# State-space scan: PSUM banks given by purpose, and a step's within-tile outputs summed last

## The reference, cut to what matters

```python
acum = jnp.cumsum(dtc * A, axis=2)                                   # running sums
Lm = jnp.exp(jnp.where(causal, acum[:, :, :, None] - acum[:, :, None, :], -jnp.inf))
CB = jnp.einsum('bnigs,bnjgs->bnijg', Cc, Bc)                        # keys times queries
y_diag = jnp.einsum('bnijg,bnijgr,bnjgr,bnjgrp->bnigrp', CB, Lm, dtc, xc)   # within the tile
ds = jnp.einsum('bnjgr,bnjgrp,bnjgs->bngrps', wj, xc, Bc)            # what the tile adds to the state
y_off = jnp.einsum('bnigs,bngrps,bnigr->bnigrp', Cc, s_prev, jnp.exp(acum)) # from the state
y = y_diag + y_off
```

## Time and profile before

| what | value |
|---|---|
| median of 3 runs | 2664.28 us (2662.90 to 2666.83) |
| the profiled execution, its own time | 2660.27 us |
| its span, first to last instruction | 2658.3 us |
| PE busy | 2324.3 us, 87% of the span |
| DVE busy | 828.9 us, 31% |
| ACT busy | 565.8 us, 21% |
| POOL busy | 96.5 us, 4% |
| mean granted TensorE clock | 0.932 of full speed |

### The profile page before, as it was taken

One profiled execution on the slowest core, in us unless ns is written; L12 is line 12 of the kernel. 1 busy time (PEld: TensorE's weight loads), 2 busy tenths in 40 slices (PEclk: granted clock), 3 DMA queues, 4 the chain that ended last, 5 costly groups with the idle time before them and its releaser, 6 DMA issues. The chain is left out here.

```text
span 2658.3 us, 35179 instructions
## 1 busy us (share of the span) xinstructions
PE 2324.3 (87%) x14554; PEld 1406.2 (53%) x14554; DVE 828.9 (31%) x1447; ACT 565.8 (21%) x1160; POOL 96.5 (4%) x64
## 2 busy tenths in 40 slices
PE   6999999999887988988479999999998779799873
PEld 3546754754555545555335466547545555455542
DVE  1255512530635222110203653125206452321002
ACT  2133301410244121000021332033102540210000
POOL 0000000100021000000000000001000210000000
PEclk8999998999988998998789999989999889899996
DMA  6321052214301215999553211331243102179993
GB/s 252 111 97 64 1 190 80 79 64 158 127 20 45 95 38 218 402 419 420 219 212 112 81 56 50 141 111 48 89 143 132 48 1 94 38 282 413 420 420 134
DMA packets 136274, 407.01 MB, mean 153 GB/s; under 512 B 9446, under 2 KB 34534, under 8 KB 125352
## 3 DMA queue, kind: packets, MB, share of 16 engines
q1 hardware_dynamic: 122600, 388.37, 38.4%
q10 hardware_dynamic: 11776, 9.97, 1.1%
q0 software_dynamic: 1728, 6.29, 0.7%
HBM read 388.59 MB, written 16.02 MB: 152 GB/s over the span
## 5 line engine op out<-in xcount | busy, mean ns | idle before, releaser
L301 PE MATMUL ps<-hT,ring 128*128 128x384 f32 x1344 | 473.3, 513 | 57.7 <-ACT arena L1524 30.6
L301 PEld LDWEIGHTS ps<-hT,ring 128*128 128x128 f32 x1344 | 268.0, 202 | 251.3 <-issue 84.1
L301 PE MATMUL ps<-ring,hT 128*128 128x512 f32 x768 | 337.1, 600 | 3.9 <-PEq L1033 3.9
L301 PE MATMUL ps<-arena,ring 128*128 128x384 f32 x768 | 253.0, 492 | 11.4 <-DVE arena L499 5.1
L301 PEld LDWEIGHTS ps<-ring,hT 128*128 128x128 f32 x768 | 147.1, 193 | 192.2 <-issue 191.6
L301 PEld LDWEIGHTS ps<-arena,ring 128*128 128x128 f32 x768 | 146.9, 192 | 115.4 <-issue 17.2
L1807 PE MATMUL ps<-ring,arena 128*32 128x256 f32 x2432 | 147.4, 405 | 30.3 <-DMA ring<-in_e_w 25.8
L1807 PE MATMUL ps<-arena 128*32 128x256 f32 x2432 | 143.9, 398 | 25.9 <-DMA arena<-in_e_w 25.9
L333 PE MATMUL ps<-cst,arena 128*128 128x128 f32 x472 | 77.6, 313 | 75.0 <-DVE arena L2086 34.4
L1807 PEld LDWEIGHTS ps<-ring,arena 128*32 128x32 f32 x2432 | 89.2, 117 | 85.0 <-issue 38.5
L1807 PEld LDWEIGHTS ps<-arena 128*32 128x32 f32 x2432 | 86.6, 115 | 78.7 <-issue 36.5
(11 more groups left out here) (293 smaller groups left out, 2456.4 us busy)
## 6 DMA issues: line engine op xcount, KB each, us to landing
ring<-in_e_w SPq DMA_DIRECT2D x48, 2048.0 KB, 15.9
arena<-in_e_w SPq DMA_DIRECT2D x48, 2048.0 KB, 17.5
ring<-in_w_in SPq DMA_DIRECT2D x36, 2048.0 KB, 7.8
ring<-in_w_ada SPq DMA_DIRECT2D x24, 2048.0 KB, 8.1
ring<-in_a_wo SPq DMA_DIRECT2D x4, 2048.0 KB, 11.6
ring<-in_b_wo SPq DMA_DIRECT2D x4, 2048.0 KB, 8.1
ring<-in_c_wo SPq DMA_DIRECT2D x4, 2048.0 KB, 8.0
ring<-in_w_out SPq DMA_DIRECT2D x4, 2048.0 KB, 7.7
```

Source lines behind the costliest of these rows:

```text
L301: ins = pe.matmul(out, a, b, start=(i == 0), stop=(i == len(pairs) - 1))
```

## The change

Every claim in the scan names its bank: the four `ai` (and, before the steps, the input states `si`) take banks 0 to 3, the gate tile of the step after bank 4, `cb` bank 5, and `ds`, `yo`, `so` (and the sums `sc`) banks 6 and 7. The two `yd` take the banks of `cb` and the gate, 5 and 4. The two gate tiles after the last step still take the next bank in turn. On DVE, `yo` moves ahead of the four masks, and the two `yd` sums move behind the state update. No instruction is added or removed.

```diff
-        def gate_pe(pe, n, key, g):
+        def gate_pe(pe, n, key, g, bank=None):
...
-            matmuls(pe, claim(pe, ((key, i), j))[:, 0:T],
+            matmuls(pe, claim(pe, ((key, i), j), bank)[:, 0:T],
...
+            B_GATE, B_CB, B_DS = 4, 5, 6
...
-                    gate_pe(pe, W_GC, "gc", 0)
+                    gate_pe(pe, W_GC, "gc", 0, B_GATE)
...
-                            transposed(pe, ("si", d, q), [ssd_in[:, d, 4 * q + i, :] for i in range(4)])
+                            transposed(pe, ("si", d, q), [ssd_in[:, d, 4 * q + i, :] for i in range(4)], 2 * d + q)
...
-                        out = claim(pe, ("sc", d))
+                        out = claim(pe, ("sc", d), B_DS + d)
...
-                        out = claim(pe, ("cb", s))
+                        out = claim(pe, ("cb", s), B_CB)
...
-                            out = claim(pe, ("ai", s, q))
+                            out = claim(pe, ("ai", s, q), q)
...
-                                pe.matmul(claim(pe, ("yo", s, g)), xbc[:, 10 + g, col],
+                                pe.matmul(claim(pe, ("yo", s, g), B_DS + g), xbc[:, 10 + g, col],
...
-                            gate_pe(pe, W_GC, "gc", s + 1)
+                            gate_pe(pe, W_GC, "gc", s + 1, B_GATE)
...
-                                pe.matmul(claim(pe, ("ds", s, g)), b_tok[:, t, g, :],
+                                pe.matmul(claim(pe, ("ds", s, g), B_DS + g), b_tok[:, t, g, :],
...
-                            out = claim(pe, ("yd", s, g))
+                            out = claim(pe, ("yd", s, g), (B_CB, B_GATE)[g])
...
-                                transposed(pe, ("so", d, q), [ssd_p[:, 512 * q + P * i:512 * q + P * i + P] for i in range(4)])
+                                transposed(pe, ("so", d, q), [ssd_p[:, 512 * q + P * i:512 * q + P * i + P] for i in range(4)], B_DS + q)
...
                         dve.wait_ge(*read(("sc", d)))
-                        for r in range(4):
-                            dve.wait_ge(*following(dve, "decayed_ready"))
-                            dve.tensor_tensor(decayed[:, 4 * r:4 * r + 4, :], quad(diff[:, r % 2, :]),
-                                              each(cbm[s % 2][:, r // 2, :], 4), ALU.mult).then_inc(*counts("mask_ready"))
-                        if s + 1 < len(SCAN):
-                            masked_keys(s + 1)
                         for g in range(G_C):
                             out = y_c[:, t, 512 * g:512 * g + 512]
                             if t:
...
-                        for g in range(G_C):
-                            out = y_c[:, t, 512 * g:512 * g + 512]
-                            dve.wait_ge(*made(("yd", s, g)))
-                            dve.tensor_tensor(out, bank(("yd", s, g)), out, ALU.add).then_inc(*reads(("yd", s, g)))
-                            dve.wait_ge(*read(("yd", s, g)))
+                        for r in range(4):
+                            dve.wait_ge(*following(dve, "decayed_ready"))
+                            dve.tensor_tensor(decayed[:, 4 * r:4 * r + 4, :], quad(diff[:, r % 2, :]),
+                                              each(cbm[s % 2][:, r // 2, :], 4), ALU.mult).then_inc(*counts("mask_ready"))
+                        if s + 1 < len(SCAN):
+                            masked_keys(s + 1)
                         if s not in LAST:
...
+                        for g in range(G_C):
+                            out = y_c[:, t, 512 * g:512 * g + 512]
+                            dve.wait_ge(*made(("yd", s, g)))
+                            dve.tensor_tensor(out, bank(("yd", s, g)), out, ALU.add).then_inc(*reads(("yd", s, g)))
+                            dve.wait_ge(*read(("yd", s, g)))
                         if t == 0:
```

## The result

The changed kernel takes 2606.24 us in the median of 4 runs (2603.20 to 2613.03), the kernel before 2663.78 of 4: ratio 0.978, interval 0.9768 to 0.9792. The forecast was 2601, within 2589 to 2622. The profiled execution took 2605.94 us, its span is 2603.7, the mean granted clock 0.938 (before 2660.27, 2658.3, 0.932).

What follows compares the result with a forecast made beforehand. A chain between engines bounds the scan: PE's gate tile waits for a bank ACT reads behind DVE's masks. Saving 31.8 us a layer, 63.6 in all, takes 2660.27 to 2596.7; plus 4.01 gives 2601 us, range 2589 to 2622.

Steps and rivals of the forecast that it cites:

- The wait: Scan, PE before the gate tile: its bank waits for ACT's reading of q = 2, behind DVE's masks; 15.3 us in three waits.
- PE's part of a step: Scan step without a stall: gate start to `yd` 9.08 us, `yd` to `yo` 3.51, `yo` 1.9; sum 14.5.
- Steps 1 and 2: First-layer scan intervals between `yd` starts: `yd` from 754.68 to 768.5 in step 1, to 784.6 in step 2.
- The copies of `so`: Scan step 2: they follow the second `yd` sum for 1.42 us and hold `yo`, 2 us of waiting moved.
- The price of the collision: DVE's `yo` additions meeting POOL's products end 0.55 us after a product; the pairs end 4.75 after the second `yd` sum.
- The last mask: Scan step 5 on DVE: over at 826.5, in time for the second half of the last `yd`.
- The rule cited from the Trainium skill: A VectorE instruction with two SBUF inputs and a GpSimd instruction reading SBUF lock each other out; without it 2590 us.
- The lower bound: No collision of additions with POOL, 0.69 us each, and last `yd` 3.7 instead of 7.06: 5.5 a layer, 2590 us.
- Rival (b): Clock stays at 1.2 GHz: gate tiles of steps 1 to 4 take 8.08 instead of 5.33 us; 2623 us, chance 0.06.
- Rival (c): Slower: late `yd` sums hold banks 4 and 5, the gate waits for DVE's whole step; 2683 us, chance 0.03.
- the rest shifts whole: After the scan, PE's gate tiles and DVE's norm start from the last `yd` as today, keeping the 63.6 us saved.
- the 4.01 us: Amount by which the median of the runs lies above the profiled execution, added to 2596.7 for 2600.7 us.

Runs made afterwards that it cites:

- the wait put back: Changed kernel plus one PE wait ahead of the gate tile, in steps 1 to 4, for ACT's reading of the running sums of q = 2: 2659.51 us.
- banks alone: Changed kernel with DVE's order put back to masks, `yo`, `yd` sums, state update; banks by purpose stay: 2637.92 us, ratio 0.9891.
- sums last alone: Kernel before, banks still in turn, with only the `yd` sums moved behind the state update: 2639.94 us, ratio 0.9903.
- mixed order: Changed kernel with `yo` ahead of the masks in steps 2 and 3 but behind them in steps 4 and 5: 2596.21 us, ratio 0.9741.

## Why the prediction was right, and where not

- **The wait.** That the gate tile's bank, and not PE's or DVE's work, set the step was right, and the wait put back shows it: 2659.5 us with everything else of the change in place. To take this wait away is not enough by itself: the banks by purpose bring in a wait of their own, of `yo` for the state update, and with banks alone that one stays (2637.9).
- **PE's part of a step**, 14.5 us: right, 14.44 in step 3. Steps 1 and 2 came at 13.77 and 16.21 for 13.8 and 16.1. The copies of `so` hold `yo` as worked out, but the wait is 0.8 us and not 2; the transposes of `so`, 1.04, are the rest of what step 2 has above 14.5.
- **DVE and POOL.** The price of the collision was right (4.80 us for 4.75), and so were its places: 1.16 us of waiting in step 4, 4.56 in step 5. The last mask was not in time for the second half of the last `yd`, which waited 0.46. That it is POOL which stretches the additions was argued from other instructions; with the addition's operand in PSUM the stretching is gone, so it is shown. The rule cited from the Trainium skill (SBUF — State Buffer, Who interferes with whom) holds here: 1.55 us with two operands in SBUF, 0.69 with one. The lower bound gave this collision 5.5 us a layer, since it let the last `yd` run fast too; without the collision that still took 7.28, and the gain was 2.0.
- **The clock.** I kept the last `yd` at 7.06; it took 7.29. Rival (b) did not come: no gate tile from step 1 on took over 5.40. The argument against it, that gate tiles were slow only behind waits of 3 us or more, does not hold everywhere: with sums last alone one took 7.08 behind 2.14 us of idle.
- **The place of `yo`.** I worked it out as part of the change but did not see that steps 4 and 5 lose by it more than steps 2 and 3 gain (75.82 against 74.03 us of stretch). Without it the whole time is the same.
- **Rival (c)**, and the rule of the Trainium skill to evacuate promptly that spoke for it (PSUM — Partial Sum Buffer, Summary: rules for kernel authors): measured, it is faster here to empty banks 4 and 5 later. With the banks apart, summing `yd` last is worth some 34 us (2638 to 2604), because banks 6 and 7, on which the next step waits, come free first. Which bank is waited for next decides here, not how soon each is emptied.
- **The whole.** The scans gave 63.0 us for the forecast's 63.6. The median fell by 57.5, and by 61.9 when both kernels were timed again. The forecast missed by 5.5 us of 2606, and not in the scan. The step that was off is "the rest shifts whole": outside the scans the changed kernel's profile is 8.4 us longer than the profile that the sum started from. Of the 4.01 us that the sum then added, from the profiled execution to the median, only 0.30 came, which makes up for part of it. Between profiles of one kernel, the one before, the same stages differ by 5.9.

## What to carry to other kernels

When PSUM banks go round in turn, a claim waits for whatever held that bank eight claims ago, and two works that have nothing to do with each other can stand in line; look in PE's waits for a releaser that belongs to another part of the step. Banks by purpose pay in full only together with the reader's order: the reader must first empty the bank that PE claims next. Each of the two edits gave 25 to 28 us alone, both together 58 to 63. And a fix of one stage is best read from that stage in the trace: here the stages around it differ by several us between executions of one kernel.

## What was not expected of the hardware

- VectorE's weighting written back into PSUM takes 0.70 us, as into SBUF (0.69).
- How much a wait costs beyond itself, and that this is not fixed by its length: gate tiles took 5.32 us with no wait, 5.40 in one layer and 7.08 in the other behind the same 2.15 us of idle (sums last alone), and 7.12 to 8.50 behind 4.36 to 5.09 (the wait put back). Behind 3.23 us of idle the last `yd` took 7.06 at a clock of 0.50 in the mixed order, and 6.20 at 0.61 behind 3.24 with the state outputs behind the masks in every step.
- Untouched stages differ between two profiles of the kernel before by up to 3.4 us, although the same stretch of a scan repeats within 0.05 us in the changed kernel. With sums last alone the scans of the two layers differ by 4.4 us.
